# Who loads and multiplies the decode keys of layer 1, and where in the shared projections their units stand

## The reference, cut to what matters

```python
s = jnp.einsum('bthe,btshe->bhts', q, kg, preferred_element_type=jnp.float32)   # dilated, 3 groups, 128 cached rows each
s = jnp.einsum('bthe,bmhe->bhtm', q, mem_kv[:, :, 0], preferred_element_type=jnp.float32)   # memory, 256 rows
```

## Time and profile before

| | |
|---|---|
| runs (3) | median 3115.38 us, 3114.88 to 3122.79 |
| profiled execution | 3119.6 us, of it the span 3117.9 |
| TensorE busy | 2917.8 us, 94% |
| VectorE, ScalarE, GpSimd busy | 51%, 36%, 15% |
| mean granted TensorE clock | 0.973 |
| key work on GpSimd | 40 operations, 51.7 us |

### The profile page before, as it was taken

How to read it: one execution, slowest core, us unless ns; L and a number is a source line. 1 busy time by engine, 2 the same in 40 slices (tenths; PEclk the granted TensorE clock), 3 DMA queues, 4 the chain that set the end, 5 groups by cost and what they waited for, 6 DMA issues and landing times. The chain is left out here.

```text
span 3117.9 us, 40698 instructions
## 1 busy us (share of the span) xinstructions
PE 2917.8 (94%) x14294; PEld 2395.4 (77%) x14294; DVE 1587.5 (51%) x3463; ACT 1126.0 (36%) x3384; POOL 461.2 (15%) x605
## 2 busy tenths in 40 slices
PE   7999999999998999979989999998999979969999
PEld 6788888887786788868767878776878769857787
DVE  4322222222234643325575766664665748766765
ACT  5211111111234234216314453521323358865642
POOL 0000000000100000000231111323221136650000
PEclk9999999999999999999999999999999989988999
DMA  4111111111134533224246656687776746656652
GB/s 146 38 41 32 32 41 31 41 30 34 65 115 149 167 129 115 86 85 145 88 188 229 234 196 231 221 263 238 253 267 220 263 162 195 203 164 202 206 156 96
DMA packets 200204, 451.82 MB, mean 145 GB/s; under 512 B 25392, under 2 KB 42352, under 8 KB 200040
## 3 DMA queue, kind: packets, MB, share of 16 engines
q1 hardware_dynamic: 172072, 367.36, 36.5%
q0 software_dynamic: 27968, 82.35, 7.0%
HBM read 333.68 MB, written 115.94 MB: 144 GB/s over the span
## 5 line engine op out<-in xcount | busy, mean ns | idle before, releaser
L109 PE MATMUL ps<-b_wp,b_sring 128*128 128x512 f32 x640 | 254.3, 397 | 26.6 <-DMA b_sring<-sums_dram 15.8
L110 PE MATMUL ps<-b_wp,b_sring 128*128 128x512 f32 x640 | 252.2, 394 | 0.0
L111 PE MATMUL ps<-b_wp,b_sring 128*128 128x512 f32 x640 | 251.9, 394 | 0.0
L109 PE MATMUL ps<-a_xthi,prepa_wh 128*128 128x512 f32 x512 | 200.0, 391 | 5.7 <-DVE prepa_wl L103 5.7
L109 PE MATMUL ps<-a_xthi,a_wh 128*128 128x512 f32 x512 | 201.0, 393 | 3.4 <-DVE a_xtlo L222 3.4
L110 PE MATMUL ps<-a_xtlo,a_wh 128*128 128x512 f32 x512 | 200.0, 391 | 0.0
L111 PE MATMUL ps<-a_xthi,a_wl 128*128 128x512 f32 x512 | 199.8, 390 | 0.0
L111 PE MATMUL ps<-a_xthi,prepa_wl 128*128 128x512 f32 x512 | 199.7, 390 | 0.0
L110 PE MATMUL ps<-a_xtlo,prepa_wh 128*128 128x512 f32 x512 | 199.6, 390 | 0.0
L109 PE MATMUL ps<-b_wp,b_xthi 128*128 128x512 f32 x480 | 187.6, 391 | 1.9 <-DVE shared_o L1703 1.9
L111 PE MATMUL ps<-b_wp,b_xtlo 128*128 128x512 f32 x480 | 187.6, 391 | 0.0
(11 more groups left out here) (414 smaller groups left out, 7386.4 us busy)
## 6 DMA issues: line engine op xcount, KB each, us to landing
b_sring<-sums_dram SPq DMA_DIRECT2D x160, 512.0 KB, 5.4
b_raws<-w_b_dram SPq DMA_DIRECT2D x176, 256.0 KB, 4.3
kv_dram<-shared_o POOLq DMA_DIRECT2D x96, 256.0 KB, 3.7
tok_b_dram<-shared_o POOLq DMA_DIRECT2D x96, 256.0 KB, 4.7
conv_raw<-w_a_dram SPq DMA_DIRECT2D x64, 256.0 KB, 3.5
sums_dram<-shared_mem SPq DMA_DIRECT2D x32, 512.0 KB, 3.3
out_grp<-grp_dram SPq DMA_DIRECT2D x48, 260.0 KB, 4.3
dil_q<-tok_b_dram SPq DMA_DIRECT2D x48, 256.0 KB, 3.3
```

The costliest lines, as they stand in the source:

```text
L109: pe.matmul(acc, a_hi, b_hi, start=first, stop=False)
L110: pe.matmul(acc, a_hi, b_lo, start=False, stop=False)
L111: return pe.matmul(acc, a_lo, b_hi, start=False, stop=last)
```

## The change

GpSimd issues the key loads itself and waits for `reduced` there. Units no longer follow a step of 7 but a list: in pair 2 at p 4 of phases 0 to 4; in pair 3 at p 0 of phases 0 to 2 (dilated), then p 0 and 4 of phases 3 and 4 (memory); in pair 4 at p 0 and 4 of phases 0 and 1 (memory). GpSimd multiplies one slab per product, at 4, 5 (and 6) positions behind the load, and VectorE reduces one position later. The load of `mem_prompt` moves from n = 224 to n = 244 (phase 2, p 4 of pair 4), and its square and scaling from phase 0 to phase 3.

```diff
-    def product(self, eng, j):
+    def parts(self, j):
+        return slabs(self.unit(j)[0])
+
+    def product(self, eng, j, part=None):
         kind, b, slab, query = self.unit(j)
-        eng.wait_ge(self.key_in[j % 4], 16 * (j // 4 + 1))
-        eng.wait_ge(self.query_in[j % 4], 16 * (j // 4 + 1))
-        for n in range(slabs(kind)):
+        if not part:
+            eng.wait_ge(self.key_in[j % 4], 16 * (j // 4 + 1))
+            eng.wait_ge(self.query_in[j % 4], 16 * (j // 4 + 1))
+        for n in range(slabs(kind)) if part is None else [part]:
             m = eng.tensor_tensor(slab[:, n, :], slab[:, n, :], query if kind == "mem" else query[:, n, :], ALU.mult)
-        m.then_inc(self.made, 1)
+        if part is None or part == slabs(kind) - 1:
+            m.then_inc(self.made, 1)
...
-        KEY0, KEY_STEP = 2 * PN, 7
+        KEYS_AT = ([2 * PN + at for at in (4, 12, 20, 28, 36)] + [3 * PN + at for at in (0, 8, 16, 24, 28, 32, 36)]
+                   + [4 * PN + at for at in (0, 4, 8, 12)])
+        key_unit = {at: u for u, at in enumerate(KEYS_AT)}
...
        @block.sync
...
-                if n >= KEY0 and (n - KEY0) % KEY_STEP == 0 and (n - KEY0) // KEY_STEP < keys.UNITS:
-                    u = (n - KEY0) // KEY_STEP
-                    if u == 0:
-                        for slot in range(RING):
-                            sp.wait_ge(o_out[slot], count(slot, CONV + 4 * SAMPLES))
-                    keys.load(sp, u)
-                if n == LASTP * PN:
+                if n == LASTP * PN + 2 * TP + 4:
                     sp.wait_ge(keys.reduced, keys.UNITS)
                     for m in range(MT):
                         sp.dma_start(mem[:, m, :], io["mem_prompt"][m * P:(m + 1) * P, :]).then_inc(mem_in[m], 16)
...
        @block.gpsimd
...
-                if n - 3 >= KEY0 and (n - 3 - KEY0) % KEY_STEP == 0 and (n - 3 - KEY0) // KEY_STEP < keys.UNITS:
-                    keys.product(pool, (n - 3 - KEY0) // KEY_STEP)
                 for i in finished_at(n):
                     store(i)
+                if n in key_unit:
+                    if n == KEYS_AT[0]:
+                        for slot in range(RING):
+                            pool.wait_ge(o_out[slot], count(slot, CONV + 4 * SAMPLES))
+                    keys.load(pool, key_unit[n])
+                for at, u in key_unit.items():
+                    if 4 <= n - at < 4 + keys.parts(u):
+                        keys.product(pool, u, n - at - 4)
...
        @block.scalar
...
-                if j == LASTP and f == 0 and p in (3, 4):
+                if j == LASTP and f == 3 and p in (3, 4):
                     mem_square(p - 3)
...
        @block.vector
...
-                u, late = divmod(n - 5 - KEY0, KEY_STEP)
-                if late == 0 and 0 <= u < keys.UNITS:
-                    keys.reduce(dve, u)
-                if j == LASTP and f == 0 and p in (4, 5):
+                for at, u in key_unit.items():
+                    if n - at == 4 + keys.parts(u):
+                        keys.reduce(dve, u)
+                if j == LASTP and f == 3 and p in (4, 5):
                     mem_scale(p - 4)
```

## The result

The changed kernel takes 3098.33 us (median of five, 3096.78 to 3102.19); the kernel before, beside it, 3117.55. The ratio is 0.9938 [0.9927, 0.9949]: 19.2 us less. 31.4 us less had been forecast, 3084.0 in a range of 3078 to 3098: the time lies just above the range.

The account below looks back on a forecast made before the run. TensorE, busy 94%, bounds the kernel; only its idle time or clock counts. -29.8 - 4.3 - 1.3 + 2.6 + 1.0 + 0.4 = -31.4 us, from a median of 3115.4 to 3084.0; range 3078 to 3098.

Parts of the forecast that it names:

- SyncE's waits are the cause: Pair 2: SyncE's three waits at key loads, 33.5 us, all go; with phases 5 and 6 cleared, 29.8 us less.
- 2020: Idle stretch of pair 2, 6.6 us, put down to sums held behind SyncE's first key wait; to go whole.
- 2115: Idle stretch of pair 2, 8.4 us, put down to SyncE's third key wait, ending at 2111; to go.
- Stretch 2095: Idle stretch of pair 2, 3.2 us, put down to SyncE's second key wait, ending at 2084; to go.
- 2145: Idle stretch of pair 2, 6.6 us, from sums queued behind a key load in phase 6; to go.
- Key loads in phases 2 ... I take 1.3 us each.: Units 2 and 7 load 1.5 MB while sums stream: 2.6 us together, range 0 to 8.6.
- the bound of 8.6: Upper price of both phase 2 key loads, 4.3 us each, if sums are held behind 1.5 MB.
- mem_prompt, "I take 0.4 us": Last pair: 1 MB ahead of a sum, landing 8.0 us against 8.2 of lead; 0.4 us, range 0 to 3.4.
- Unit 4 into phase 5, 1.0 us: Unit 4's product opens phase 5 with stores behind it, phase 4 stores sharing its queue; 1.0 us, range 0 to 3.2.
- Issues on GpSimd, cost 0: GpSimd issues 32 loads, 0.5 or 1.6 us for each 384-row issue; stays hidden, cost 0.
- GpSimd's waits: GpSimd waits for reductions and key landings, stores behind; landings within 11.7 us, output ring and PSUM banks cover late stores.
- (c): Rival: GpSimd becomes late, landings of about 23 us stall TensorE; slower, 3120 us. Chance 0.08.

Follow-up runs that it names:

- e1: The changed kernel, but SyncE issues the key loads at the new places: ratio 1.0008 to the kernel before, pair 2 at 188.2 us.
- e2: GpSimd issues the key loads in the old step of 7, three slabs multiplied at once, later mem_prompt load kept: ratio 0.995 to the kernel before, pair 2 186.0 us.
- e3: The changed kernel with the loads of units 2 and 7 (phase 2) cut to 16 rows, scores from old data: ratio 0.9900 to the kernel before.
- e4: The changed kernel with mem_prompt loaded a phase later (n = 253), square and scaling in phase 4: pairs 3 and 4 0.4 us shorter.
- e6 to e8: Three variants of the changed kernel: smaller memory units in phases 2 with mem_prompt late; loads spread over positions; both. Ratios to the kernel before 0.9917 to 0.9925.

## What the forecast had right, and the steps that failed

*SyncE's waits are the cause.* They are a cause; that they were nearly all of it isn't shown. Take pairs 2 to 4 together. At the new places it costs 27.0 us if SyncE issues (e1, 523.8 against 496.7); at the old steps GpSimd as the issuer saves 14.2 of 518.1 (e2). But the 27.8 us of pair 2 come only with both parts of the change: the issuer alone takes off 9.8, the places alone 7.6.

The kernel before shows why. In only one of the five stretches of the earlier trace rows, 2020, does TensorE stand for nothing but a sum that a SyncE wait had held back. The largest, 2115, ends with two waits at once: TensorE's timeline, VectorE's, and the landing of GpSimd's store of 2112.86.

```profile
2123.36 0.76 PE L109 MATMUL ps<-b_wp,b_sring 128*128 128x512 f32 x1 [7.72 <-DVE shared_o L1566]
```

```profile
2122.61 0.69 DVE L1566 TENSOR_TENSOR shared_o<-ps,b_spare 128x512 f32<-128x512 f32 x1 [3.87 <-DMA kv_dram<-shared_o]
...
DMA to landing us min/median/max: 9.7/9.7/9.7
```

That store went out without delay, behind the key load of 2111.4, landed at 2122.6, and only then had VectorE a slot. The sum that SyncE had issued late, at 2112.36, landed after 10.9 us, at 2123.3. Taking away one of the two would have gained nothing there. Stretch 2095 is alike: VectorE stood until 2096.8 for the store of 2086.85 (9.9 us to land), and of the 2.6 us idle only 0.4 is a wait on a sum. The prediction had put both stretches down to SyncE's second and third wait and the sums behind them. It missed that outputs, too, stand behind the keys. Its result for them still came out, of 2020, 2115 and 2145 nothing is left, because the new places keep key loads out of phases 5 and 6. So as far as it was reckoned from SyncE's waits, it came right in part by luck.

*"Key loads in phases 2 ... I take 1.3 us each."* This is the step that failed, by its size: a landing behind 1.5 MB was priced as if the other queue partly shielded the sums. The two loads cost 2.74 and 3.03 us of idle time with slow matmuls behind the second, 5.9 us in e3's profile and 7 to 12 in its timing: nearer the bound of 8.6 than the 2.6 taken. I had said that the rows lean neither way on whether another queue protects the sums. It doesn't: 10.7 and 11.0 us to land., where GpSimd's stores waited as long as SyncE's queue was full, had said so in the other direction, and I should have taken it at its word.

*mem_prompt, "I take 0.4 us".* The second step that failed: 2.7 us idle (window 2375). The landing was sized rightly, 8.0 us worked out and 7.2 to 8.5 seen for the four sums behind it. The lead wasn't: a sum has 8.2 us only if SyncE issues it as its slot comes free. The one that TensorE stood for (it landed at 2377.6, and TensorE goes on at 2377.7; the profile itself names no releaser), needed at 2375.0, could have gone out at 2366.8 and went out at 2370.41, as SyncE stood at the raw weights until 2369.1 and then issued them and mem_prompt: 3.6 + 7.2 - 8.2 = 2.6. I had looked at SyncE's wait for keys there and not at its other waits.

*Unit 4 into phase 5, 1.0 us.* 1.67 us idle at 2095; near, but by another wait: 1.47 of it is for a sum, and the forecast had priced the stores. The 0.57 us at 2025, behind unit 1, weren't in the sum.

*Issues on GpSimd, cost 0.* Right: 0.76 to 0.84 us for 384 rows, hidden. *GpSimd's waits:* the query rows land within 12.1 us, near the 11.7 reckoned with; (c) stopped TensorE nowhere in the changed kernel.

The sum again with what the profiles show: pair 2 keeps 6.3 us where 2.3 were forecast, pairs 3 and 4 grow by 6.4 where 0.4 were; 10.0 us in all, and -31.4 + 10.0 = -21.4, the difference of the spans. The terms above make up 6.9 of the 10.0: the phases 2 5.9 - 2.6, mem_prompt 2.7 - 0.4, unit 4 0.7, and 0.6 at 2025. The other 3.1 us are laid to no term; pairs 3 and 4 have 2.2 us more of busy time (321.11 against 318.94), matmuls slowed behind the stalls among them. Rival (b), contention only moved, kept 15.2 us; the trace kept 35.4 - 21.4 = 14.0. The time is (b)'s: 3098.3 against its 3095 and the forecast's 3084, just above the range. What stayed is contention, as (b) has it, with each of its three prices somewhat too high. Against (b) I had set that the sums are again issued ahead of the keys. That holds for the first four of a phase 2 and not for those that refill a slot, which are the ones that stood.

## What to carry to other kernels

Moving a large load to another engine's queue takes away the issuer's waits, and nothing of the transfer: price what streams beside it at the landing time seen behind such a load before (10.8 to 11.6 us here), against the lead of its buffer (8.2 us). Do it for the outputs too: a stall that the profile lays to VectorE can be a store that hasn't landed. And before a stall is put down to one wait, look whether a second ends at the same time. Two loads of equal bytes can land after 7 or 9 us (medians here) by where their rows are read from, so look at the landing times of each source before you move a load in time; here the copy of a broadcast row into one contiguous row was worth 6.5 us, while no other placing or splitting of the loads (e4, e6 to e8) was clear of the changed kernel. A load split in the program is split in time only where its engine is held back there.

## What the runs showed of the hardware

None of the theories had expected the following. The same 768 KB of query land (median of eight loads in one profile each, issued by GpSimd) after 9.4 to 9.5 us from three broadcast rows of 2 KB 4.2 MB apart, 8.1 us from three 4 KB apart, 7.1 to 7.5 us from one row of 6 KB that all 128 partitions read, 8.4 us from 384 different rows, and 9.2 to 9.4 us when sixteen copies serve eight partitions each, near or far. Issued by SyncE in the kernel before they took 9.6 us, and from 384 different rows 7.1.

Stores of 256 KB that GpSimd issued just behind a key unit landed after 8.7 to 9.7 us in the kernel before (2112.9 to 2116.6) and 12.9 us in e2; the one of 2110.0, ahead of the unit, took 2.3.

GpSimd's issue of such a load took 0.76 to 0.86 us for 384 rows of 2 KB, 0.70 to 0.80 for 256, and 0.54 to 0.60 us for 128 rows of 6 KB, as for its stores of 128 rows of 2 KB (0.52 to 0.61): three times the bytes at the same number of rows cost nothing more.
